# Expert weights of an fp32 mixture-of-experts layer as the stationary operand, in plain fp32, in place of split fp32r passes with the tokens stationary

## What is computed

```
affinity = softmax(xt @ w_router)
gates, idx = top_k(affinity.T, cap)       # cap = 64 of the sample, 32 of the prompt: 96 rows per expert
xe  = xt[ids]                             # 96 x 1024
hdn = silu(xe @ wg) * (xe @ wu)           # wg, wu: 1024 x 2816
ye  = (hdn @ wd) * g[:, None]             # wd: 2816 x 1024
out[idx] += ye
```

## Time and profile before

| | us |
|---|---|
| median of 3 runs | 2142.48 (2139.83 to 2146.63) |
| the profiled execution | 2141.78 |
| its span in the trace | 2140.0 |
| PE, PE loads, DVE, ACT, POOL busy | 2053.1, 1491.9, 1660.3, 1294.4, 182.7 |
| granted clock of TensorE, mean | 0.981 |

### The profile page before, as it was taken

The page is one execution under the profiler, slowest core; times in us unless marked ns, Lnnn a source line. Parts: engine busy times, 40 slices in busy tenths (PEclk is TensorE's granted clock), DMA queues, the critical chain, the costliest instruction groups (busy, mean ns, idle before and its releaser), DMA issues.

```text
span 2140.0 us, 27211 instructions
## 1 busy us (share of the span) xinstructions
PE 2053.1 (96%) x9878; PEld 1491.9 (70%) x9878; DVE 1660.3 (78%) x1346; ACT 1294.4 (60%) x1131; POOL 182.7 (9%) x118
## 2 busy tenths in 40 slices
PE   6999999989769999999999999999999999999996
PEld 5766767678647777777777777777777777777775
DVE  4533857673558888888888888888888888888887
ACT  4213312551247777777777777777777777777775
POOL 1000312200020101010010101001010100101000
PEclk9999999999879999999999999999999999999998
DMA  7225214313559999999999999999999999999994
GB/s 198 93 104 187 74 67 146 137 71 136 199 202 371 359 389 366 382 370 373 381 366 389 366 382 369 376 379 371 385 364 385 369 380 373 372 384 366 385 366 183
DMA packets 310264, 637.60 MB, mean 298 GB/s; under 512 B 19272, under 2 KB 83144, under 8 KB 308682
## 3 DMA queue, kind: packets, MB, share of 16 engines
q1 hardware_dynamic: 306506, 624.00, 80.4%
q0 software_dynamic: 3712, 12.98, 2.5%
HBM read 610.20 MB, written 26.74 MB: 298 GB/s over the span
## 4 chain that ended last, share of the span: by engine, by line
PE 89%; DVE 6%; issue 2%; ACT 2%; DMA 2%; POOL 0%; SPq 0%; DVEq 0%; POOLq 0%; ACTq 0%
PE bank L922 22%; PE bank L920 22%; PE bank L921 22%; PE bank L647 5%; PE bank L854 3%; PE bank L727 3%; PE bank L658 2%; PE bank L781 2%; PE bank L737 2%; PE bank L959 1%; DVE ysum_sample L1414 1%; PE bank L756 1%; PE bank L768 1%; ACT split_ring L1230 1%; PE bank L705 1%
## 5 line engine op out<-in xcount | busy, mean ns | idle before, releaser
L1666 DVE TENSOR_TENSOR split_ring<-breg,split_ring 128x2048 fp32r<-128x2048 f32 x525 | 1202.1, 2290 | 199.3 <-ACT split_ring L1230 199.3
L1230 ACT CAST split_ring<-breg 128x2048 fp32r<-128x2048 f32 x525 | 1004.4, 1913 | 399.9 <-PE bank L922 399.9
L920 PE MATMUL bank<-split_ring,xe_split 128*96 128x512 f32 (+1 forms) x1536 | 582.8, 379 | 1.6 <-DVE xe_split L1677 1.6
L922 PE MATMUL bank<-split_ring,xe_split 128*96 128x512 f32 (+1 forms) x1536 | 579.1, 377 | 0.0
L921 PE MATMUL bank<-split_ring,xe_split 128*96 128x512 f32 (+1 forms) x1536 | 575.0, 374 | 0.0
L922 PEld LDWEIGHTS bank<-split_ring,xe_split 128*96 128x96 f32 x1536 | 248.2, 162 | 90.6
L921 PEld LDWEIGHTS bank<-split_ring,xe_split 128*96 128x96 f32 x1536 | 249.3, 162 | 86.3
L920 PEld LDWEIGHTS bank<-split_ring,xe_split 128*96 128x96 f32 x1536 | 248.7, 162 | 85.8 <-DVE xe_split L1677 1.9
L920 PE MATMUL bank<-split_ring,ht_split 128*96 128x512 f32 x704 | 277.7, 394 | 1.7 <-DVE ht_split L1684 1.5
L922 PE MATMUL bank<-split_ring,ht_split 128*96 128x512 f32 x704 | 276.8, 393 | 0.0
L921 PE MATMUL bank<-split_ring,ht_split 128*96 128x512 f32 x704 | 276.1, 392 | 0.0
(11 more groups left out here) (217 smaller groups left out, 1688.7 us busy)
## 6 DMA issues: line engine op xcount, KB each, us to landing
breg<-in_w_down SPq DMA_DIRECT2D x176, 1024.0 KB, 7.0
breg<-in_w_up SPq DMA_DIRECT2D x175, 1024.0 KB, 7.2
breg<-in_w_gate SPq DMA_DIRECT2D x174, 1024.0 KB, 6.5
w_raw<-in_w_in SPq DMA_DIRECT2D x24, 512.0 KB, 4.1
filter_spectra<-kf_out SPq DMA_DIRECT2D x6, 1024.0 KB, 5.5
kf<-filter_spectra SPq DMA_DIRECT2D x6, 1024.0 KB, 6.3
w_out_raw<-in_w_out SPq DMA_DIRECT2D x4, 1024.0 KB, 6.4
bias<-in_attn_bias SPq DMA_DIRECT2D x8, 448.0 KB, 5.3
```

The costliest lines, as they stand in the source:

```text
L920: pe.matmul(out, x_hi, w_hi, start=start, stop=False)
L922: return pe.matmul(out, x_lo, w_hi, start=False, stop=stop)
L1230: act.copy(sp_unit[n % SPLIT_RING][0], raw[slot]).then_inc(hi_done, 1)
L1666: dve.tensor_tensor(sp_unit[s][1], raw[later_place(n, e)[0]], sp_unit[s][0].bitcast(F32), ALU.subtract).then_inc(lo_done, 1)
```

## The change

The weights become the stationary operand, 128 by 128 numbers at a time, and the tokens (xT) or hidden values (hT), 96 columns, move. Both are plain fp32: hi_part, lo_part, three_passes, multiply_last, the split rings and the splitting of tokens and hidden values go. The products come out with channels on the partitions, so that turn_hidden goes as well, and the expert's result is turned once at its end (yT, turn_out: eight transposes). silu and h are made in that layout on 128 partitions. The 48 KB per partition of split_ring and 8 KB of breg hold seven more raw units (LATE_EXTRA), which are filled once before the first expert; after that the ring has 11 slots as before, and SP waits for unit_mm in place of lo_done. PE itself waits for the load of each unit (raw_in). The first expert stands ahead of the loop, which runs experts 1 to 14. POOL's three low parts and its copy of the first index column go, too, and the last rows' norms stand earlier in the last expert.

```diff
-EXTRA = 3
-RAW_RING, SPLIT_RING = 11, 3
-ALL_SLOTS = RAW_RING + EXTRA
+EXTRA, LATE_EXTRA = 3, 7
+RAW_RING = 11
+FIRST_LAP = EXTRA + RAW_RING
+ALL_SLOTS = FIRST_LAP + LATE_EXTRA
...
-    return (n - EXTRA) % RAW_RING, (n - EXTRA) // RAW_RING + 1
+    if n < FIRST_LAP:
+        return n - EXTRA, 1
+    if n < ALL_SLOTS:
+        return RAW_RING + EXTRA + n - FIRST_LAP, 1
+    return (n - ALL_SLOTS) % RAW_RING, (n - ALL_SLOTS) // RAW_RING + 2
 
 
 def raw_before(n):
 
-    return n - RAW_RING
+    return n - ALL_SLOTS + EXTRA if n < ALL_SLOTS + RAW_RING else n - RAW_RING
...
-        split = region("split_ring", 48, 48, F32R)
-
-        xe_split = region("xe_split", 8, 6, F32R)
-        ht_split = region("ht_split", 14, 3, F32R)
+        sreg = region("sreg", 48, 48)
...
-        xeT = [xe_split[:, part * KD * SLOTS:(part + 1) * KD * SLOTS].rearrange("p (k s) -> p k s", k=KD)
-               for part in range(2)]
-        hsT = [ht_split[:, part * 4 * SLOTS:(part + 1) * 4 * SLOTS].rearrange("p (j s) -> p j s", j=4)
-               for part in range(2)]
-        h_now = view(xreg, 17, (512,), SLOTS)
-        silu = view(xreg, 19, (512,), SLOTS)
+        xT = view(xreg, 8, (KD, SLOTS))
+        hT = [view(xreg, 11 + 1.5 * s, (4, SLOTS)) for s in range(2)]
+        silu = view(xreg, 14, (4, SLOTS))
+        yT = view(xreg, 15.5, (KD, SLOTS))
...
+            for n in (FIRST_LAP - 1, FIRST_LAP):
+                load_unit(n, *unit_at(n))
...
+            sp.wait_ge(xn_out, 32 * TILES)
+            sp.wait_ge(logit_mm, TILES)
+            for n in range(FIRST_LAP + 1, ALL_SLOTS):
...
-                    sp.wait_ge(lo_done, e * UNITS_PER_EXPERT + (raw_before(n) + 1))
+                    sp.wait_ge(unit_mm, e * UNITS_PER_EXPERT + (n - RAW_RING + 1))
...
-            def three_passes(out, x_hi, x_lo, w_hi, w_lo, start, stop):
-
-                pe.matmul(out, x_hi, w_hi, start=start, stop=False)
-                pe.matmul(out, x_hi, w_lo, start=False, stop=False)
-                return pe.matmul(out, x_lo, w_hi, start=False, stop=stop)
-
...
-            def multiply(n, kind, c, part, count):
-
-                w_hi, w_lo = (by_rows(sp_unit[n % SPLIT_RING][half], kind, c) for half in range(2))
-                pe.wait_ge(lo_done, count + 1)
+            def multiply(n, kind, c, part, e, half_done=None):
+
+                slot, uses = later_place(n, e)
+                laps = UNITS_PER_EXPERT // RAW_RING
+                pe.wait_ge(raw_in[slot], e * (16 * laps) + 16 * uses)
+                unit = by_rows(raw[slot], kind, c)
                 if kind == "d":
-                    for j in range(2):
-                        jj = 2 * part + j
-                        for half in range(2):
-                            mm = three_passes(bank[4 + half][0:SLOTS, :], hsT[0][:, jj, :], hsT[1][:, jj, :],
-                                              w_hi[:, j, half * W:(half + 1) * W], w_lo[:, j, half * W:(half + 1) * W],
-                                              c == 0 and jj == 0, c == CHUNKS - 1 and jj == 2 * PARTS[c] - 1)
+                    for half in range(2):
+                        for j in range(2):
+                            jj = 2 * part + j
+                            for d in range(4):
+                                mm = pe.matmul(cols(4 + half, 4, SLOTS)[:, d, :],
+                                               unit[:, j, (4 * half + d) * P:(4 * half + d + 1) * P], hT[c % 2][:, jj, :],
+                                               start=(c == 0 and jj == 0 and d == 0),
+                                               stop=(c == CHUNKS - 1 and jj == 2 * PARTS[c] - 1),
+                                               skip_group_check=True)
+                        if half_done is not None:
+                            mm.then_inc(half_done, 1)
+                    if half_done is not None:
+                        return
                 else:
-                    out = bank["gu".index(kind)][0:SLOTS, 0:WIDTHS[c]]
-                    rows = KD // PARTS[c]
+                    rows, blocks = KD // PARTS[c], 2 * PARTS[c]
                     for k in range(rows):
                         kk = part * rows + k
-                        mm = three_passes(out, xeT[0][:, kk, :], xeT[1][:, kk, :], w_hi[:, k, :], w_lo[:, k, :],
-                                          kk == 0, kk == KD - 1)
+                        for f in range(blocks):
+                            mm = pe.matmul(cols("gu".index(kind), 4, SLOTS)[:, f, :], unit[:, k, f * P:(f + 1) * P],
+                                           xT[:, kk, :], start=(kk == 0 and f == 0), stop=(kk == KD - 1),
+                                           skip_group_check=True)
                 mm.then_inc(unit_mm, 1)
 
-            def turn_hidden(c, done):
-
-                pe.wait_ge(h_done, done + 1)
-                for j in range(2 * PARTS[c]):
-                    mm = pe.transpose(cols(2, 4, SLOTS)[:, j, :], h_now[:, j * P:(j + 1) * P],
-                                      ident[0:SLOTS, 0:SLOTS])
-                mm.then_inc(h_turned2, 1)
-
-            def expert(e, last=False):
-
-                count, n = e * UNITS_PER_EXPERT, LEAD
+            def turn_out(count):
+
+                for half, copied in enumerate((y_act, y_dve)):
+                    pe.wait_ge(copied, count)
+                    for d in range(4):
+                        mm = pe.transpose(cols(2 + half, 4, P, SLOTS)[:, d, :], yT[:, 4 * half + d, :], ident[:, :])
+                    mm.then_inc(y_turned, 1)
+
+            def expert(e, first=False, last=False):
...
+                            pe.wait_ge(xe_act, e + 2)
+                            pe.wait_ge(xe_dve, e + 2)
                         pe.wait_ge(silu_done, m)
                         for part in range(PARTS[after]):
-                            multiply(n, "g", after, part, count + n)
+                            multiply(n, "g", after, part, e)
                             n += 1
+                        if c == 0 and not first:
+                            turn_out(e)
                         pe.wait_ge(h_done, m)
                         for part in range(PARTS[after]):
-                            multiply(n, "u", after, part, count + n)
+                            multiply(n, "u", after, part, e)
                             n += 1
                     if c == CHUNKS - 2 and not last:
                         pe.wait_ge(gathered, e * 16 + 32)
-                        pe.wait_ge(xe_done, e + 1)
                         turn_in()
-                    if c == 0:
-                        pe.wait_ge(ysc_done, e * 2 + 2)
-                    pe.wait_ge(hs_done, m)
...
                     for part in range(PARTS[c]):
-                        multiply(n, "d", c, part, count + n)
+                        multiply(n, "d", c, part, e, None if more else half_mm)
                         n += 1
-                    turn_hidden(after, m)
 
             pe.sem_inc(xe_mm, 2)
+            pe.sem_inc(y_turned, 2)
             pe.wait_ge(gathered, 16)
             turn_in()
-            pe.wait_ge(xe_done, 1)
-            pe.wait_ge(lo_done, SPLIT_RING)
+            pe.wait_ge(xe_act, 1)
+            pe.wait_ge(xe_dve, 1)
             for n in range(LEAD):
                 kind, c, part, _ = unit_at(n)
-                multiply(n, kind, c, part, n)
-            turn_hidden(0, 0)
-            with pe.Fori(0, EXPERTS - 1) as e:
+                multiply(n, kind, c, part, 0)
+            expert(0, first=True)
+            with pe.Fori(1, EXPERTS - 1) as e:
                 expert(e)
             expert(EXPERTS - 1, last=True)
+            turn_out(EXPERTS)
...
-            def hi_part(n, e):
-
-                slot, uses = later_place(n, e)
-                laps = UNITS_PER_EXPERT // RAW_RING
-                act.wait_ge(raw_in[slot], e * (16 * laps) + 16 * uses)
-                if n >= SPLIT_RING:
-                    done = e * UNITS_PER_EXPERT + (n - SPLIT_RING + 1)
-                    act.wait_ge(unit_mm, done)
-                act.copy(sp_unit[n % SPLIT_RING][0], raw[slot]).then_inc(hi_done, 1)
-
-            def tokens_hi(count):
-                for half in range(2):
-                    act.wait_ge(xe_mm, count * 2 + 1 + half)
-                    act.copy(xeT[0][:, 4 * half:4 * half + 4, :], cols(6 + half, 4, SLOTS)).then_inc(xe_hi, 1)
-
-            def hidden_hi(c, count):
...
+            def tokens_first(count):
+                act.wait_ge(xe_mm, count * 2 + 1)
+                act.copy(xT[:, 0:4, :], cols(6, 4, SLOTS)).then_inc(xe_act, 1)
 
             def gate_silu(c):
-                act.activation(silu[:, 0:WIDTHS[c]], bank[0][0:SLOTS, 0:WIDTHS[c]], ACT.Silu).then_inc(silu_done, 1)
-
-            def expert(e, last=False):
+                blocks = 2 * PARTS[c]
+                act.activation(silu[:, 0:blocks, :], cols(0, 4, SLOTS)[:, 0:blocks, :], ACT.Silu).then_inc(silu_done, 1)
...
```

(119 more changed lines are left out.)

117 lines of the change are left out of this document (25 added, 92 removed).

## The result

The changed kernel takes 2621.22 us (median of 4 runs, 2620.05 to 2622.35) against 2141.57 before, a ratio of 1.223 with a 95% interval of 1.2212 to 1.2249. The forecast was 2543 with a range of 2505 to 2640: the direction and the main term held, and 78 us are missing.

The account below looks back on a forecast made before the run. PE was taken as the bound, the DMA 8% below it. Start 605.9, pairs 1884, turnings 10 and 13, cold start 2, loop 13 and end 14 gave a 2542 span, 2543 us forecast, range 2505 to 2640.

Parts of the forecast that it names:

- The pace: PE's expert matmuls: 16896 load and matmul pairs, set by the 128-column load at 0.1115 us each, 1884 us.
- The loop body: PE's jump back, 13 times, with about 2144 records per expert: 1 us each, 13 us, bounds 0 to 50.
- fetch rival: PE's loop body is fetched again at a full 8.9 us wait per jump: 116 us instead of 13, 2645; 9%.
- 1884 + 10 + 13 + 2: PE's expert part in us: pairs 1884, turn_in 10, turn_out 13, cold start 2.
- The faster one: Rival: load hidden or faster, pace below 0.088 us, the DMA becomes the bound, about 2040 us; 5%.
- Load and stream: Rival: PE's load and stream partly in series, 0.138 us a pair (near 2990) or 0.120 (2687); 8% for both.
- the 2% I gave it: Clock rival: the array falls to its 1.2 GHz level, pairs at 0.22 us, about 4370 us; 2%.
- The start: Before the experts: faster cast, POOL's splitting gone, slower gather; first weighted matmul at 605.9 us instead of 608.5.
- 4.6 written: The gather at the start lands under traffic of six more queued units: 8.9 us for 4.28, +4.6.
- The end: From the last matmul to the end: 14 us, against 14.5 before.
- The work taken from ACT and DVE: ACT and DVE lose their whole splitting work, which buys nothing, since PE did not wait for it.
- the seven slots: Seven extra ring slots buy nothing: the loads need 293 GB/s, and 374 flowed before.

Follow-up runs that it names:

- straight-code kernel: The changed kernel with PE's loop over experts 1 to 14 written out as straight code: 2532.31 us, ratio 1.1836 to the kernel before.
- run 6: The changed kernel with PE's loop written out, and without the seven late slots (LATE_EXTRA 7 to 0): 2532.94 us, ratio 1.1826 to the kernel before.

## Why the prediction was right, and where it was short

**The pace: right.** 16896 pairs at 0.1115 were 1884 us. The changed kernel's 900 in 100 us and the straight-code kernel's 5388 in 600 us, turnings included, are 0.111. That the load sets it was argued from 16 and 64 columns. One pace with 64, 96 and 128 columns shows that the stream does not; that the load does is what is left, and no run changed the load. Why transposes, whose loads have 128 columns as well, go at 0.082 stays open.

**The loop body: the step that failed.** I wrote "I take 1 us each, 13", because the old loop jumps without loss. The old loop is held and says nothing of one that is not. Measured are 87.8 us (the changed kernel less the straight-code one), 6.75 a jump: 47.5/13 = 3.7 us idle, and the rest, some 3 us, at half clock behind it (2.8 at the seam shown). Of the 76 us by which the span 2617.9 exceeds my 2542, this term is 75. It lies outside its own bounds of 0 to 50, and 2621 is just past the 2620 that these bounds gave: the time fell into the stated range because that was widened to take in most of the fetch rival. The rival with the full wait of 8.9 us (116) had the right mechanism and was nearer in size; it had no clock in it, and the idle time was under half of the wait that it took, so that its size was nearer by two errors that cancel in part. The instruction count, 2144 against 900, was in the text, and the instruction queue was the right thing to look for.

**What agreed in part by luck.** Without the loop term the sum is 2529, and the straight-code kernel's span is 2530.1. Its first weighted matmul came at 603.4, 2.5 sooner than forecast, and from there to the end of its last it took 1912.6 us, 3.6 more than the 1884 + 10 + 13 + 2; the two nearly cancel.

**The rivals.** The faster one needed a pace under 0.088 and met 0.111. Load and stream do not add. The DMA had room, 298 GB/s. In the changed kernel's stream of experts the clock fell only around the stalls, but the runs with 64 and 80 columns show that the 2% I gave it was thin: a kernel a little narrower would have paid 126 us, or at 64 columns with the loop 1460 (4081 against 2621).

**The start and the end.** 605.9 was forecast and 602.8 measured: the cast fell to 0.17 us as written, the gather went out 8 us sooner and lost 3.1 us to the loads (4.6 written). Of the 3.1 us that this is better than the forecast, 1.6 are the offset that this trace had already at 562 us. With the same work ahead, run 6 shows one of 6.5 us, so that these 1.6 are luck. The end took 2617.9 - 2603.8 = 14.1 us against 14, its table load of 1.28 us included. The work taken from ACT and DVE bought nothing, as written, and neither did the seven slots, which run 6 shows.

## What to carry to other kernels

When fp32 weights of 128 columns are the stationary operand and few columns move, count pairs of load and matmul and price each by the load: from 64 to 128 moving columns a pair cost the same 0.111 us here, so that a narrow moving side is paid in full. Splitting one operand so that it can move 512 wide at one pass each was cheaper here (2.77 us a unit against 32 x 0.1117 = 3.57), although it looks like three times the work and keeps two more engines busy. Count the instructions in a loop body before writing a loop: a jump is free only for a body that the engine still holds, and the idle us at a jump can cost the clock as well.

## What the runs showed that was not expected

A loop body of some 1103 instructions on PE drew no instruction traffic, and bodies of some 1631, 1895 and 2160 were fetched again in each pass, with 7.7, 4.1 and 3.7 us of idle time a jump (100.7, 52.7 and 47.5 over 13). At 64 and 80 moving columns PE ran busy for 270 us at a granted clock of 0.50, and with 64 columns and stalls it stayed there from 1120 us to the end (4081 us in place of 2621), with the same instructions per unit as the 96-column kernel. No kernel of these runs that computes the whole layer beats the one before; the change with straight code is 18.4% slower (1.1816 to 1.1856), and with the seven slots left out besides it is the same.
